# Retention's two value units of a head as one pass of 512-column products over four weight slots

## The reference

```python
def _retention(q, k, v):            # 4 heads, q and k 256 wide, v 512 wide
    ...
    scores = einsum(q, k) * decay
    o_inner = einsum(scores, v)     # and a carried state; together a causal product
    ...
    return (o - mu) * rsqrt(var + GN_EPS)

p = h @ w_in                        # rq, rk, rv, rg, ... = split(p)
y_ret = _retention(_rotary(rq), _rotary(rk), rv)
y_a = (silu(rg) * y_ret) @ w_ret_out

c_act = silu(c)
mod = c_act @ w_ada[l] + b_ada[l]   # computed meanwhile, on DVE, for later norms
```

## Time and profile before

| what | value |
|---|---|
| median of 3 runs | 2314.2 us |
| the profiled execution | 2315.32 us, span 2313.6 us |
| granted TensorE clock, mean | 0.998 of full speed |
| PE busy | 2286.9 us, 99% of the span |
| DVE, ACT, POOL busy | 1084.1, 907.3, 1142.4 us |
| chain that ended last | PE 92%, DVE 5%, DMA 1%, ACT 1% |

### The profile page before, as it was taken

How to read it: one execution, slowest core, us unless ns; L and a number is a source line. 1 busy time by engine, 2 the same in 40 slices (tenths; PEclk the granted TensorE clock), 3 DMA queues, 4 the chain that set the end, 5 groups by cost and what they waited for, 6 DMA issues and landing times.

```text
span 2313.6 us, 30107 instructions
## 1 busy us (share of the span) xinstructions
PE 2286.9 (99%) x12138; PEld 1927.2 (83%) x12138; DVE 1084.1 (47%) x1503; ACT 907.3 (39%) x1093; POOL 1142.4 (49%) x1489
## 2 busy tenths in 40 slices
PE   7999999999999999999999999999999999999998
PEld 4888888888888888888898888888888788888887
DVE  5776657546653341122276756441666534221223
ACT  4332233256675242232333323232666834332332
POOL 3454544544455555555554455445444454545552
PEclk9999999999999999999999999999999999999999
DMA  9444534322222323323344444222222222323321
GB/s 295 138 152 145 180 119 146 128 73 74 73 92 73 103 89 103 98 92 99 102 146 135 148 146 132 96 73 91 81 73 72 68 96 87 109 91 91 108 92 55
DMA packets 244153, 252.48 MB, mean 109 GB/s; under 512 B 4016, under 2 KB 241728, under 8 KB 244032
## 3 DMA queue, kind: packets, MB, share of 16 engines
q1 hardware_dynamic: 242496, 247.53, 33.2%
q10 hardware_dynamic: 1536, 3.17, 0.5%
HBM read 248.59 MB, written 2.10 MB: 108 GB/s over the span
## 4 chain that ended last, share of the span: by engine, by line
PE 92%; DVE 5%; DMA 1%; ACT 1%; issue 0%; DVEq 0%; SPq 0%; ACTq 0%
PE proj L877 69%; PE proj L914 10%; PE att L1012 2%; PE proj L899 2%; PE att L1058 2%; PE att L1068 1%; PE att L1046 1%; DVE slab L1187 1%; PE proj L941 1%; PE att L992 1%; DVE att L1294 1%; DVE h_lo L1301 1%; PE att L1021 1%; DMA slab<-in_w_ada 1%; PE att L941 0%
## 5 line engine op out<-in xcount | busy, mean ns | idle before, releaser
L390 POOL TENSOR_TENSOR w_lo<-w_raw,w_hi 128x256 fp32r<-128x256 f32 x1472 | 1140.3, 807 | 1137.3 <-ACT w_hi L436 1136.7
L877 PE MATMUL proj<-h_hi,w_hi 128*128 128x512 f32 x1568 | 617.8, 394 | 0.3 <-DVE work L1357 0.2
L877 PE MATMUL proj<-h_hi,w_lo 128*128 128x512 f32 x1568 | 611.2, 390 | 0.0
L877 PE MATMUL proj<-h_lo,w_hi 128*128 128x512 f32 x1568 | 610.6, 389 | 0.0
L436 ACT ACTIVATE w_hi<-w_raw 128x1024 fp32r<-128x1024 f32 (+1 forms) x374 | 385.9, 1040 | 524.3 <-PE proj L877 443.9
L877 PEld LDWEIGHTS proj<-h_hi,w_lo 128*128 128x128 f32 x1568 | 294.3, 188 | 62.4
L877 PEld LDWEIGHTS proj<-h_hi,w_hi 128*128 128x128 f32 x1568 | 294.5, 188 | 62.1 <-issue 2.4
L877 PEld LDWEIGHTS proj<-h_lo,w_hi 128*128 128x128 f32 x1568 | 294.7, 188 | 59.0
L877 PE MATMUL proj<-y_hi,w_lo 128*128 128x512 f32 x800 | 311.3, 389 | 0.0
L877 PE MATMUL proj<-y_hi,w_hi 128*128 128x512 f32 x800 | 311.3, 389 | 0.0
L877 PE MATMUL proj<-y_lo,w_hi 128*128 128x512 f32 x800 | 311.3, 389 | 0.0
(11 more groups left out here) (224 smaller groups left out, 2460.1 us busy)
## 6 DMA issues: line engine op xcount, KB each, us to landing
w_raw<-in_w_in SPq DMA_DIRECT2D x88, 1024.0 KB, 5.1
slab<-in_w_ada SPq DMA_DIRECT2D x42, 1024.0 KB, 8.1
w_raw<-in_w_up SPq DMA_DIRECT2D x32, 1024.0 KB, 5.7
w_raw<-in_w_down SPq DMA_DIRECT2D x32, 1024.0 KB, 5.1
w_raw<-in_w_ret_out SPq DMA_DIRECT2D x16, 1024.0 KB, 5.5
w_raw<-in_w_sb_out SPq DMA_DIRECT2D x8, 1024.0 KB, 5.1
w_raw<-in_w_mix_out SPq DMA_DIRECT2D x8, 1024.0 KB, 5.2
first_y<-in_w_ada SPq DMA_DIRECT2D x4, 1024.0 KB, 12.0
```

What stands on the lines that cost most here:

```text
L390: ins = pool.tensor_tensor(w_lo[:, s, ks, :], w_raw[:, s // 2, ks, P * (s % 2):P * (s % 2 + 1)], w_hi[:, s, ks, :], ALU.subtract)
L877: last = pe.matmul(proj[:, j, :], w[:, slot, k, :], a[:, k, :], start=k == 0 and n == 0, stop=k == KT - 1 and n == 2)
```

## The change

- `v_units` takes both value units in one pass: for each k and each of four token tiles, three products whose moving side is `w[:, :, k, :]`, all four slots, 512 columns. Each token tile has a bank of its own (`v_of`): tiles 0 and 1 in `att[4]` and `att[5]`, tiles 2 and 3 in `proj`. There are 96 products of 512 columns for 192 of 256.
- The four slots come free together, at the end of the pass. So the split is counted in halves of k: unit k's products run in two halves of k (`first_unit(..., (KH, KH), k_used)`), and the splits of u+3, u+4 and u+5 are made in halves of k behind `k_used` and `v_used`. `low_order` lists in which order POOL and the counts go; POOL's loop becomes straight code.
- On DVE the four `low_v` (now one for each token tile, in the order 2, 3, 0, 1) stand behind all four `sum_ada`. PE waits for `v_taken` ahead of `add_ada`.
- The second product of the rotation goes into a buffer of its own, `rot_too`, which takes a wait out of the six operations.

```diff
-LO_CREDIT = 4
+LO_CREDIT = 8
+def low_order(layer):
+    order, pair = [], layer * LAYER_PAIRS
+    for unit in range(LAYER_UNITS):
+        head_unit = unit % (2 * RET_PAIRS) if unit < SB_FIRST else 2 * RET_UNITS
+        at = head_unit % RET_UNITS if head_unit < 2 * RET_UNITS else 0
+        if at == 3:
+            order += [(unit, j, ks) for ks in K_HALVES for j in range(2)]
+        elif at == 4:
+            order += [(unit + n, j, ks) for ks in K_HALVES for n in range(2) for j in range(2)]
+        elif at != 5:
+            order += [(unit, j, WHOLE) for j in range(2)]
+    return order
...
+        def v_of(t):
+            return att[:, 4 + t, :] if t < 2 else proj[:, t - 2, :]
...
                 s = unit % 2
-                sp.wait_ge(lo_ready, 4 * pair + 2 * unit - 2 + LO_CREDIT)
+                late = 2 if unit in BEHIND_V else 0
+                sp.wait_ge(lo_ready, 8 * pair + 4 * unit - 4 + late + LO_CREDIT)
...
+                        for kh in range(2):
+                            if kh == 0:
+                                act.wait_ge(k_used, head + 1)
+                            else:
+                                products(pair, u + 1, 1)
                             for half in range(2):
+                                split_half(pair, u + 3, half, kh)
...
-                        for unit in (u + 2, u + 3):
+                        act.wait_ge(v_used, head + 1)
+                        for unit in (u + 4, u + 5):
                             for half in range(2):
-                                products(pair, unit, half)
...
-                            for half in range(2):
-                                split_weights(pair, unit + 2, half)
+                                split_half(pair, unit, half, 0)
+                        products(pair, u + 3, 1)
+                        for half in range(2):
+                            split_half(pair, u + 4, half, 1)
+                        for t in (2, 3, 0, 1):
+                            act.activation(v_hi[:, t, :], v_of(t), ACT.Copy).then_inc(v_half, 1)
+                        for half in range(2):
+                            split_half(pair, u + 5, half, 1)
...
+            def v_units(pair, unit):
+                for kh in range(2):
+                    pe.wait_ge(lo_ready, 8 * pair + 4 * (unit + 1) + 2 * (kh + 1) + LO_CREDIT)
+                    for k in range(KH * kh, KH * (kh + 1)):
+                        for t in range(TB):
+                            if k == 0 and t in (0, 3):
+                                pe.wait_ge(bank_free[t // 2], 2 * pair + unit + 1)
+                            for n, (w, a) in enumerate(((w_hi, h_hi), (w_lo, h_hi), (w_hi, h_lo))):
+                                last = pe.matmul(v_of(t).rearrange("p (a n) -> p a n", a=4),
+                                                 a[:, k, t * P:(t + 1) * P], w[:, :, k, :],
+                                                 start=k == 0 and n == 0, stop=k == KT - 1 and n == 2)
+                            if k == KT - 1:
+                                last.then_inc(proj_done, 1)
+                    if kh == 0:
+                        last.then_inc(v_used, 1)
...
-                        whole_unit(pair, u + 1, h_hi, h_lo)
-                        token_unit(pair, u + 2)
-                        token_unit(pair, u + 3)
+                        first_unit(pair, u + 1, h_hi, h_lo, None, (KH, KH), k_used)
+                        v_units(pair, u + 2)
...
                         half_unit(pair, u + 4, 0, h_hi, h_lo)
+                        pe.wait_ge(v_taken, 2 * head + 2)
...
                         for q in range(4):
                             if has_ada(layer, i, h):
                                 sum_ada(layer, i, ADA_BATCH * h + q)
-                            low_v(q)
+                        for n, t in enumerate((2, 3, 0, 1)):
+                            low_v(n, t)
```

More of the change, by code:

```diff
@@ L177, in hybrid_trunk @@
         rot = part(7680, SEQ)
+        rot_too = part(P_AT, SEQ)
         gated_t = rot
@@ L250, in hybrid_trunk @@
         hi_ready, lo_ready = sem("hi_ready"), sem("lo_ready")
+        k_used, v_used, v_taken = sem("k_used"), sem("v_used"), sem("v_taken")
         proj_done = sem("proj_done")
@@ L383, in _ @@
             pool.sem_inc(lo_ready, LO_CREDIT)
[L384 to L392, removed]
+            counted = 0
+            for layer in range(DEPTH):
+                for unit, j, ks in low_order(layer):
+                    s, slot = unit % 2, 2 * (unit % 2) + j
+                    counted += (ks.stop - ks.start) // KH
+                    pool.wait_ge(hi_ready, counted)
+                    for k in range(ks.start, ks.stop, 2):
+                        ins = pool.tensor_tensor(w_lo[:, slot, k:k + 2, :], w_raw[:, s, k:k + 2, P * j:P * (j + 1)],
+                                                 w_hi[:, slot, k:k + 2, :], ALU.subtract)
+                    ins.then_inc(lo_ready, (ks.stop - ks.start) // KH)
         @block.scalar
@@ L868, in half_unit @@
                 slot = 2 * (unit % 2) + j
-                pe.wait_ge(lo_ready, 4 * pair + 2 * unit + j + 1 + LO_CREDIT)
+                behind = BEHIND_HALVES[j].get(unit, 0)
+                pe.wait_ge(lo_ready, 8 * pair + 4 * unit + 2 * (j + 1) + behind + LO_CREDIT)
                 pe.wait_ge(bank_free[j], 2 * pair + unit + 1)
@@ L883, in whole_unit, with first_unit @@
                     half_unit(pair, unit, j, hi, lo, tile_ready if j == 0 else None)
-            def first_unit(pair, unit, hi, lo, tile_ready, steps):
+            def first_unit(pair, unit, hi, lo, tile_ready, steps, used=None):
                 k0 = 0
@@ L902, in first_unit @@
                             last.then_inc(proj_done, 1)
+                        elif used is not None and j == 1:
+                            last.then_inc(used, 1)
                     k0 += step
+            def v_units(pair, unit):
[13 more added lines that the diff above has]
+                        last.then_inc(v_used, 1)
             def token_unit(pair, unit):
                 slot = 2 * (unit % 2)
-                pe.wait_ge(lo_ready, 4 * pair + 2 * unit + 2 + LO_CREDIT)
+                pe.wait_ge(lo_ready, 8 * pair + 4 * unit + 4 + LO_CREDIT)
                 for t in range(TB):
```

54 lines of the change are left out of this document (33 added, 21 removed).

## The result

The changed kernel takes 2347.3 us (median of 4 runs, 2344.6 to 2348.7) where the kernel before takes 2314.1 in the same comparison: a ratio of 1.014, 95% interval 1.0128 to 1.0151. The forecast was 2335, with a range of 2315 to 2348. The sign and the mechanism were right; the price was 33 us where I had 20, and the measured time lies 0.7 us under the upper end of the range. The profiled execution is the slowest of the four (2348.7 us, mean granted clock 0.989; the fastest has 2344.6 us and 0.994).

The account below looks back on a forecast made before the run. PE bounds the kernel, busy 99%, with DVE only 0.2 us off the chain. Passes -10.4, waits +25.2, older waits -0.5 and clock +6 give +20.3 on 2314.2: forecast 2335 us, range 2315 to 2348.

Parts of the forecast that it names:

- part 1: PE's value pass: 96 products of 512 columns for 192 of 256 save 1.3 us a head, 10.4 in eight.
- parts 2 and 3: Inputs of the value pass and POOL's split weights for gate half (u+4, 0) are ready in time: no cost.
- part 4: Bank `proj[0]`, emptied by `low_v` behind four DVE sums: PE waits 3.6 us in seven heads, +25.2 us.
- part 5: PE's granted clock falls after the new idle: 1.2 us in five of seven heads, 6 us; bounds 0 to 12.
- The sum: Whole kernel: passes -10.4, waits +25.2, older waits of heads 3 and 6 -0.5, clock +6, together +20.3 us.
- The end of the range: Upper limit for the whole kernel, 2348 us: full price of the clock with PE's wait at 4.4 us.
- The clock holds: Rival: PE waits as forecast but the granted clock does not fall, without the 6 us: 2328 us; chance 0.24.
- almost in time: Rival: fourth unit lands early, DVE's sum meets less of POOL, PE waits 1.5 us a head: 2314; chance 0.10.
- Full gain: Rival: neither bank nor weights hold PE, so the whole 10.4 us is gained: 2304 us; chance 0.05.
- No faster pass: Rival: the 512-column value pass equals two of 256; 10.4 us gone, wait 1.3 shorter a head: about 2336; chance 0.06.
- POOL last: Rival: u+5 lands late, so POOL's weights for slot (u+4, 0) come after DVE: 2342 us; chance 0.05.

Follow-up runs that it names:

- experiments 2: Kernel before with each `w_ada` sum of the value stretches cut to one of eight operations, modulation values incomplete: 2313.8 us, ratio 0.9998.
- experiment 1: Changed kernel with each `w_ada` sum of the value stretches cut to one of eight operations, modulation values incomplete: 2303.5 us, ratio 0.9952.
- experiment 3: Changed kernel plus 15 unread 512-column products between scores and gate half in the seven heads with sums: 2334.5 us, ratio 1.0087.
- experiment 5: Changed kernel with the third and fourth `w_ada` units loaded only in half, modulation values wrong: 2325.9 us, ratio 1.0045.
- experiment 4: Changed kernel with the four `low_v` moved on DVE ahead of the fourth `w_ada` sum: 2327.3 us, ratio 1.0061.
- experiment 7: Changed kernel, full result: fourth sum behind the scores' low halves, `low_v` behind the third, small products in the second gate half: 2303.5 us, ratio 0.9953.
- experiment 6: Changed kernel with POOL making only every other subtraction for the gate units, low halves partly stale: 2337.6 us, ratio 1.0099.

## Why the forecast was right, and where it was short

**The products (part 1).** -10.4 us forecast, -10.3 between experiments 2 and 1, -1.3 in the last head. Right, and the extra of 13.4 ns is by the product: with four pieces the rate is still 226.7 ns. The Trainium skill's 2.5 ns a matmul (TensorE: Matmul & The Clock Gate, section "Wait — 56ns, not 53.3ns?") would have given an estimated 1.9 us; neither of the two streams of products here comes near it.

**Banks and weights (parts 2 and 3).** Costed at nothing, and nothing: in experiment 1 PE goes through the pass and into the gate half without idle. The 86.4 for POOL's weights of u+4 against PE's 86.35 looked tight and was mis-sized. In head 0 of the changed kernel the load of u+5 landed 7.8 us after its issue for my 9.1, and POOL began its twelve instructions at 79.46 for my 81.6 (of these 2.1 us 0.8 are an earlier start of the whole pass). By `low_order` the fifth and sixth are those of slot (u+4, 0):

```profile
L423 POOL TENSOR_TENSOR w_lo<-w_raw,w_hi x2: 737/830/922, 82.5 to 83.2; 128x256 fp32r<-128x256 f32 x2
```

They end at 84.1, and PE was through its scores at 85.5, so there too the weights were 1.4 us early.

**The bank behind the sums (part 4).** Right in place, releaser and course: the third sum alone, the idle for the DMA (1.93 us for my 2.1), the fourth sum slow throughout (7.1 us for my 6.5, since the first of its eight operations is slow beside POOL as well, 0.91 for 0.34). In head 0 PE waited 4.0 us for 3.6. The sum of seven was mis-sized, 29.3 us for 25.2. Heads 3 and 6 hold 2.8 of the 4.1 us: there PE waited 5.3 and 4.7, since the fourth unit landed 7.4 and 6.9 us after its issue. I had put the landing at 6.1 because the load of u+6 would not be beside it. It was not beside it, and in these two heads the landing was late all the same; the mean of the seven is 6.2.

**The clock (part 5).** This is the term that failed most. I had 1.2 us in five of seven heads, 6 us. It fell in all seven, and the gate halves took between 7.33 and 8.20 us for 5.50; experiment 3 puts 12.8 to 14.4 us on it, over my upper bound of 7 x 1.7 = 12. The step that failed is the length of a fall: the row I took the price from the earlier trace rows had 1.7 us lost in one, but in the changed kernel the clock came back later. From 86 to 98 us of head 0 the windows have 4 x 0.32 + 4 x 0.50 + 4 x 0.03 = 3.4 us lost. The first of these figures puts the fall at some 87.4 us, so 1.0 of the 3.4 went into idle time and 2.4 into the products. That a part lies in the idle time was right (I had allowed 0.5); the stretch was twice as long. And "it did not fall after an idle of 2.2 us" had one case behind it; experiment 5 has falls with four of seven idles of 2.3, experiment 4 with two of seven of 2.5. Idles of one length had both outcomes, and what decides between them was not tried.

**The sum.** In the profiled executions, 2347.0 against 2313.6 of span: the passes -10.4, the waits +29.3, the older waits -0.5, the clock +14.4 (experiment 3, profiled) give 32.8 for 33.4. The end of the range was added up too high: the wait at 4.4 us and the full price of the clock are 2314.2 - 10.9 + 30.8 + 12 = 2346, not 2348. By that sum the measured 2347.3 lies outside, so that it fell inside the stated range is luck.

**The rivals.** "The clock holds" is what experiment 3 brings about, 2334.5 with the longer waits, not 2328. Experiment 5 comes nearest to "almost in time", with waits of 2.3 us for 1.5 and four falls; it takes half of the bytes away to get there. "Full gain" is experiment 1. "No faster pass" and "POOL last" are out by experiment 1, and in the changed kernel itself each of the eight passes takes 21.8 us.

## What to carry to other kernels

When a change merges two steps that each freed a buffer into one that frees it at the end, look at what the freeing engine does between: work that was spread between the two moves ahead of the single hand-over, and an engine that was 0.2 us off the chain becomes it. Put on the freeing engine first what someone waits for, and background work (here the last sum, 4 to 7 us) where nobody is behind it: `low_v` moved ahead of the fourth sum took 20 of the 33 us away (experiment 4), and the fourth sum moved behind the scores, with its small products, made it -11 (experiment 7). And price an idle of TensorE at more than its length: here each idle of 3.3 to 5.3 us was paid with another 1.8 to 2.7 in slow products.

## What the runs showed of the hardware

- **The granted clock** fell with idles of 2.3 us in four of seven cases (experiment 5), of 2.5 in two of seven (experiment 4), and in all seven both of 2.6 to 3.3 us (experiment 6) and of 3.3 to 5.3 (the changed kernel); it held in all seven heads of experiment 3, with idles of 1.5 us or less. In the changed kernel a fall cost 1.8 to 2.7 us in the 24 products behind it, in head 0 of experiment 6 3.1 (8.6 for 5.5).
- **DVE beside POOL.** A 128x256 operation with two SBUF inputs takes 0.49 us alone and 0.84 beside POOL's, as before; new is that the tensor-by-scalar form with one tensor input is slowed as well, 0.91 us beside POOL (head 0 of the changed kernel) for 0.34 with POOL at rest (experiment 7). With half of POOL's instructions for the gate units gone the fourth sum fell from 7.1 to 5.5 us.
- **Landing of a 1 MB load** issued with another under way is not fixed by its issue: 5.8 and 7.4 us in two heads of one execution; issued 0.7 us earlier it arrived 0.7 later (experiment 6). Why heads 3 and 6 are the slow ones before and after was not tried and stays open.
